# Selecting the top 256 keys of a row: a bitwise threshold search in place of rounds of eight maxima, inside a TensorE-heavy streaming encoder step

## What is computed

```python
def dsa_attend(q, qi, wi, k_all, v_all, ki_all, mask, n_sel):
    dots = einsum('bqhd,bsd->bqhs', qi, ki_all) * (D_I ** -0.5)
    score = einsum('bqh,bqhs->bqs', wi, relu(dots))
    if mask is not None:
        score = where(mask, score, NEG_BIG)
    _, sel = lax.top_k(score, n_sel)          # n_sel = 256 for the prompt
    ...                                        # attention over the selected keys only
```

## Time and profile of the kernel before

| | |
|---|---|
| runs shown | 3953.46, 3950.20, 3951.51 us |
| median | 3951.51 us |
| span of the profiled execution (first to last instruction) | 3929.5 us |
| median less span | 22.0 us |
| PE, DVE, ACT, POOL busy | 3692.2, 2321.4, 1128.6, 758.1 us |
| DVE in L1604 and L1605 (all rounds, both halves) | 367.4 and 359.9 us, plus 92 ns for each value load |

### The profile page before, as it was taken

The page is one execution under the profiler, slowest core; times in us unless marked ns, Lnnn a source line. Parts: engine busy times, 40 slices in busy tenths (PEclk is TensorE's granted clock), DMA queues, the critical chain, the costliest instruction groups (busy, mean ns, idle before and its releaser), DMA issues. The chain is left out here.

```text
span 3929.5 us, 54494 instructions
## 1 busy us (share of the span) xinstructions
PE 3692.2 (94%) x21676; PEld 2935.9 (75%) x21676; DVE 2321.4 (59%) x4713; ACT 1128.6 (29%) x2672; POOL 758.1 (19%) x812
## 2 busy tenths in 40 slices
PE   7997899999999999999999998999989999899998
PEld 5765577787877667778767787887766777688887
DVE  1664566498963664549556554488955565554542
ACT  1124333211124442321234332111134443322221
POOL 2300220301101232220100015312000101453334
PEclk9998899999999999999999999999999999999999
DMA  4331223412212222342312123343221212342223
GB/s 146 97 113 58 83 90 95 137 52 78 84 51 75 69 88 84 105 124 81 96 63 73 60 66 116 114 115 110 73 80 40 77 38 67 87 145 86 65 82 96
DMA packets 151606, 339.55 MB, mean 86 GB/s; under 512 B 30184, under 2 KB 68648, under 8 KB 138040
## 3 DMA queue, kind: packets, MB, share of 16 engines
q1 hardware_dynamic: 91576, 291.04, 23.7%
q10 hardware_dynamic: 59776, 45.02, 3.9%
HBM read 299.33 MB, written 36.68 MB: 86 GB/s over the span
## 5 line engine op out<-in xcount | busy, mean ns | idle before, releaser
L901 PE MATMUL PS<-xn,wring 128*128 128x272 f32 (+1 forms) x7168 | 1682.0, 394 | 33.9 <-DVE xn L1527 11.7
L901 PEld LDWEIGHTS PS<-xn,wring 128*128 128x128 f32 x7168 | 1374.8, 194 | 298.4 <-issue 37.4
L1859 POOL TENSOR_TENSOR xT<-xT,res 128x272 f32<-128x272 f32 (+1 forms) x320 | 253.9, 795 | 2302.9 <-ACT res L1184 2254.8
L901 PE MATMUL PS<-dense,wring 128*128 128x256 f32 (+1 forms) x2816 | 662.7, 394 | 11.9 <-DVE dense L1509 6.3
L901 PEld LDWEIGHTS PS<-dense,wring 128*128 128x128 f32 x2816 | 537.6, 194 | 111.5 <-issue 10.9
L1604 DVE MAX8 top<-scr 128x8 f32<-128x384 f32 (+6 forms) x418 | 367.4, 879 | 12.2
L1605 DVE MATCH_REPLACE8 scr<-top,scr 128x384 f32<-128x384 f32 (+6 forms) x418 | 359.9, 861 | 0.0
L1184 ACT ACTIVATE res<-PS 128x272 f32<-128x272 f32 (+1 forms) x320 | 123.2, 387 | 587.0 <-PE PS L901 565.4
L922 PE MATMUL PS<-wring,xn 128*128 128x256 f32 (+1 forms) x1152 | 267.9, 392 | 4.0 <-ACT dense L1198 4.0
L922 PEld LDWEIGHTS PS<-wring,xn 128*128 128x128 f32 (+1 forms) x1152 | 213.1, 187 | 53.6 <-issue 8.8
L901 PE MATMUL PS<-catT,wring 128*128 128x272 f32 (+1 forms) x1024 | 231.5, 387 | 5.3 <-issue 2.7
(11 more groups left out here) (199 smaller groups left out, 4113.2 us busy)
## 6 DMA issues: line engine op xcount, KB each, us to landing
wring<-in_wu SPq DMA_DIRECT2D x88, 1024.0 KB, 4.9
wring<-in_wf SPq DMA_DIRECT2D x88, 512.0 KB, 3.7
wring<-in_wo SPq DMA_DIRECT2D x64, 512.0 KB, 3.7
wring<-in_wd SPq DMA_DIRECT2D x96, 320.0 KB, 2.9
wring<-in_wd SPq DMA_DIRECT2D x64, 384.0 KB, 3.1
wring<-in_wn SPq DMA_DIRECT2D x16, 1024.0 KB, 5.3
kv<-out_projT ACTq DMA_DIRECT2D x48, 256.0 KB, 4.1
out_projT<-dense SPq DMA_DIRECT2D x40, 272.0 KB
```

Source lines behind the costliest of these rows:

```text
L901: mm = nc.tensor.matmul(PS[:, dbank(t.g0), 0:cw], wtile(t.q, i), rhs, start=(kk == a), stop=(kk == b - 1))
L1859: nc.gpsimd.tensor_tensor(x, x, res[:, i % NRES, 0:cw], ALU.add).then_inc(s_res, 1)
```

## The change

For half 1 only (m = 1 and m = 3) the pick steps go, and with them all 128 rounds of L1604 and L1605 of a stage; half 0 keeps them. The steps of X for half 1 become: load, dots, then near and far of all four units after each other (the dots of the next unit now in the "far" step; the scores are accumulated straight into the `bias` tile, so that all four units' scores lie there together), "sign", 31 steps "bit", four steps "last".

"sign" counts, for each row, the scores at or above 0 and so settles whether the 256th largest value is negative; the row is multiplied by -1 if so, and the goal count is set. The 31 "bit" steps then find the threshold's fp32 pattern: eight for the exponent, by multiplying the candidate by powers of two, and 23 for the mantissa. In each, units 0 and 1 (640 and 768 keys) are counted by DVE (a compare with the candidate and a sum, in one instruction), units 2 and 3 (896 and 1024 keys) by ACT (the sign of score minus candidate, summed along the row). DVE moves all candidates. "last" sets a last mantissa bit for the far units, restores signs, settles ties with a running count (a scan), and writes the bias. Step "bit" 15 carries the loads of stage B. `bmask`, an unused constant, makes room for `halves`, the powers 2^-1 to 2^-23.

```diff
+EXPONENTS = (127, 63, 32, 16, 8, 4, 2, 1)
+MANTISSA = 23
+BITS = len(EXPONENTS) + MANTISSA
+ON_DVE = 2
...
 def _pick_steps(h):
     out = [("load", 0, 0), ("dots", 0, 0)]
+    if h == 1:
+        for y in range(len(PICKS[h])):
+            out += [("near", y, 0), ("far", y, 0)]
+        return out + [("sign", 0, 0)] + [("bit", b, 0) for b in range(BITS)] + [("last", y, 0) for y in range(len(PICKS[h]))]
...
-ATT_LOAD = [("pick", len(PICKS[h]) - 1, 2) for h in range(2)]
+ATT_LOAD = [("pick", len(PICKS[0]) - 1, 2), ("bit", BITS // 2, 0)]
...
         for what, y, z in PICK_STEPS[h]:
-            k = PICKS[h][y].nk / 1000
+            k = PICKS[h][min(y, len(PICKS[h]) - 1)].nk / 1000
             if what == "load":
                 out.append((0, 0.5, 0, 14))
+            elif what == "sign":
+                out.append((0, 0, 6, 0))
+            elif what == "bit":
+                out.append((0, 3, 3.5, 0))
+            elif what == "last":
+                out.append((0, 0, 10 * k, 0))
...
@@ idx_tensor @@
-                elif what == "pick" and z == 6 and y + 1 < len(PICKS[h]):
+                elif what == ("far" if h == 1 else "pick") and z == (0 if h == 1 else 6) and y + 1 < len(PICKS[h]):
                     dots(y + 1, 0)
...
@@ idx_scalar @@
+                elif what == "bit":
+                    act.wait_ge(x_cand, BITS * (m // 2) + y + 1)
+                    for i in range(ON_DVE, len(PICKS[1])):
+                        u = PICKS[1][i]
+                        ins = nc.scalar.activation(rl[:u.w, i - ON_DVE, 0:u.nk], bias[:u.w, u.bias:u.bias + u.nk], ACT.Sign, bias=cand[:u.w, i:i + 1],
+                                                   accum_out=count[:u.w, i:i + 1])
+                    ins.then_inc(x_cnt, 1)
...
@@ idx_vector @@
+            def count_from(i, bound):
+                u = PICKS[1][i]
+                return nc.vector.tensor_scalar(work[:, 0:u.nk], kept(u), bound, None, ALU.is_ge, ALU.add, accum_out=count[:, i:i + 1])
+
+            def move(b, part):
+                c, hit = cand[:, part], sel[:, part]
+                step(nc.vector.tensor_tensor(hit, count[:, part], goal[:, part], ALU.is_ge))
+                e = b - len(EXPONENTS)
+                if e < 0:
...
+                    step(nc.vector.tensor_scalar(hit, hit, yes - no, no, ALU.mult, ALU.add))
+                    last = nc.vector.tensor_tensor(c, c, hit, ALU.mult)
...
+                    return last
+                step(nc.vector.scalar_tensor_tensor(hit, hit, 0.5 if e < MANTISSA - 1 else 1.0, steps_of[:, e, part], ALU.subtract, ALU.mult))
+                return nc.vector.tensor_tensor(c, c, hit, ALU.add)
...
+                elif what == "bit":
+                    if y:
+                        dve.wait_ge(x_cnt, bits + y)
+                        move(y - 1, far).then_inc(x_cand, 1)
+                    for i in range(ON_DVE):
+                        step(count_from(i, cand[:, i:i + 1]))
+                    step(move(y, near))
+                elif what == "last":
+                    if y == 0:
+                        dve.wait_ge(x_cnt, bits + BITS)
+                        step(move(BITS - 1, far))
...
+                        for i in range(ON_DVE, 4):
+                            step(count_from(i, sel[:, i:i + 1]))
...
+                    step(nc.vector.tensor_scalar(x, x, sign[:, y:y + 1], None, ALU.mult))
+                    step(nc.vector.tensor_scalar(work[:, 0:u.nk], x, bound, None, ALU.is_gt, ALU.add, accum_out=count[:, y:y + 1]))
+                    step(nc.vector.tensor_scalar(same, x, bound, None, ALU.is_equal))
+                    step(nc.vector.tensor_scalar(least[:, y:y + 1], count[:, y:y + 1], -1.0, float(TOP_P), ALU.mult, ALU.add))
+                    step(nc.vector.tensor_tensor_scan(rank, same, same, 0.0, ALU.add, ALU.max))
+                    step(nc.vector.scalar_tensor_tensor(same, rank, least[:, y:y + 1], same, ALU.is_gt, ALU.mult))
+                    step(nc.vector.scalar_tensor_tensor(rank, x, bound, same, ALU.is_lt, ALU.add))
+                    nc.vector.tensor_scalar(x, rank, 8 * NEG, None, ALU.mult).then_inc(x_bias, 1)
```

More of the change, by code:

```diff
@@ L497, in build @@
         ident, mean, hmean = sb("ident", [P, P]), sb("mean", [P, P]), sb("hmean", [P, P])
-        lmask, bmask = sb("lmask", [P, NL, 32]), sb("bmask", [P, 4, 32])
+        lmask, halves = sb("lmask", [P, NL, 32]), sb("halves", [P, MANTISSA, 4])
+        steps_of = sb("steps_of", [P, MANTISSA, 4])
+        cand, count, least, goal, sign, sel = (sb(n, [P, 4]) for n in ("cand", "count", "least", "goal", "sign", "sel"))
         epst, fgain = sb("epst", [P, 1]), sb("fgain", [P, KD])
@@ L552, in build @@
         x_in, x_dots, x_relu, x_acc, x_bias = sem("x_in"), sem("x_dots"), sem("x_relu"), sem("x_acc"), sem("x_bias")
+        x_cand, x_cnt = sem("x_cand"), sem("x_cnt")
         s_kv = [sem("s_kv0"), sem("s_kv1")]
@@ L751, in load_rest @@
             def load_rest():
-                for t, name in ((par, "params"), (fgain, "fgain"), (clow, "clow"), (ident, "ident"), (lmask, "lmask"), (bmask, "bmask"),
+                for t, name in ((par, "params"), (fgain, "fgain"), (clow, "clow"), (ident, "ident"), (lmask, "lmask"), (halves, "halves"),
                                 (hmean, "hmean")):
@@ L1582, in idx_vector, with kept @@
                     step(nc.vector.memset(bias[0:64, u.bias + u.nk - 64:u.bias + u.nk], 8 * NEG))
+            def kept(u):
+                return bias[:u.w, u.bias:u.bias + u.nk]
+            def count_from(i, bound):
[6 more added lines that the diff above has]
+                if e < 0:
+                    up = EXPONENTS[b + 1] if e < -1 else 0
+                    yes, no = 2.0 ** up, 2.0 ** (up - EXPONENTS[b])
+                    step(nc.vector.tensor_scalar(hit, hit, yes - no, no, ALU.mult, ALU.add))
+                    last = nc.vector.tensor_tensor(c, c, hit, ALU.mult)
+                    if e == -1:
+                        step(last)
+                        w = part.stop - part.start
+                        step(nc.vector.tensor_tensor(steps_of[:, :, part], halves[:, :, part], c.unsqueeze(1).to_broadcast([P, MANTISSA, w]), ALU.mult))
+                        last = nc.vector.tensor_tensor(c, c, steps_of[:, 0, part], ALU.add)
+                    return last
+                step(nc.vector.scalar_tensor_tensor(hit, hit, 0.5 if e < MANTISSA - 1 else 1.0, steps_of[:, e, part], ALU.subtract, ALU.mult))
+                return nc.vector.tensor_tensor(c, c, hit, ALU.add)
+            near, far = slice(0, ON_DVE), slice(ON_DVE, 4)
+            bits = BITS * (m // 2)
             for what, y, z in PICK_STEPS[h]:
-                u = PICKS[h][y]
-                wk = work[:u.w, 0:u.nk]
+                u = PICKS[h][y] if what not in ("bit", "sign") else None
                 if what in ("near", "far"):
+                    wk = kept(u) if h == 1 else work[:u.w, 0:u.nk]
                     for hh in range(2):
@@ L1592, in idx_vector @@
                             dve.wait_ge(x_in, 16 * sum(IX_LOADS[i % 2] for i in range(m + 1)))
-                            dve.wait_ge(x_bias, sum(len(PICKS[i % 2]) for i in range(m)) + y)
+                            dve.wait_ge(x_bias, sum(len(PICKS[i % 2]) for i in range(m)) + (y if h == 0 else 0))
                             nc.vector.tensor_scalar(wk, rl[:u.w, hh, 0:u.nk], iw[:u.w, u.slot, 0:1], None, ALU.mult).then_inc(x_acc, 1)
@@ L1600, in idx_vector @@
                         if u.prompt:
-                            step(nc.vector.memset(work[0:64, u.nk - 64:u.nk], NEG))
+                            step(nc.vector.memset(wk[0:64, u.nk - 64:u.nk], NEG))
                 elif what == "pick":
+                    wk = work[:u.w, 0:u.nk]
                     for r in range(BURST * z, min(BURST * z + BURST, ROUNDS[h][y])):
```

33 lines of the change are left out of this document (31 added, 2 removed).

## The result

The change makes the kernel faster, by about twice what was forecast: a ratio of **0.9904, 95% interval 0.9882 to 0.9926**, 3904.32 us (median of four runs, 3898.34 to 3917.21) beside 3950.86 in the same rounds. The two medians alone would give 0.988, on the edge of that interval. Forecast was 3932, about 0.995; the median lies just under the low end of the range, 3908. Rows of "before" stand above and are named by their group.

What follows compares the result with a forecast made beforehand. TensorE (PE), busy 94% of the span, bounds the kernel. B and C gaps -20, old X losses -17, new ones +18 make -19 us: span about 3910, plus 22.0 to the median, 3932; range 3908 to 3980.

Steps and rivals of the forecast that it cites:

- I let idle and clock loss shrink in proportion to steps per turn: B1, C1, B3, C3: more dense turns between steps win back 2.8, 4.0, 6.3 and 7.3 us, together 20.
- I take half: B1, C1, X3, B3, C3: half of (1 - clock) x length counted as loss, 3.0 to 6.2 us each, the rest overlapping idle.
- Rival 4: B and C: gaps shrink to the bound of 45 us, giving 3907; chance 0.09.
- X, -17 + 18: X1 and X3: old losses of 17 us go, new ones of 18 come, bounds 5 and 60.
- the old losses: X1 and X3: PE idle of 3.9 and 9.1 us and 3.8 for X3's clock, 17 us, all to go.
- (b): FFN tiles and bits of X: ACT waits for DVE in each bit; 7 us of PE idle, 3 for the clock.
- The 22.0 us between span and median: Whole kernel: 22.0 us added to the forecast span of about 3910 to reach a median of 3932.
- Rival 1: B and C gaps stay as chains within a step, X gives back its win: -1 +/- 7 us, 3950; chance 0.17.
- Rival 2: Bits of X: copies of dense tiles held up behind ACT's counts cost 56 us, net +37, 3988; chance 0.22.
- Rival 3: ACT in X1: sign needs another activation table than tanh, 16 more loads, 21 us on ACT, 3947; chance 0.05.

Runs made afterwards that it cites:

- repeat of the change: The changed kernel run once more with no edit, beside the kernel before in the same rounds: 0.9886 [0.9864, 0.9908], 3902.33 us.
- before again: The kernel before run once more with no edit, for a second profiled execution: 3949.2 us, span 3947.3.

## Why the prediction was partly right

The sign and the mechanism were right: PE's time, not DVE's, is the measure; X's lighter work is worth nothing by itself in the sum of both layers; the gain comes from more dense turns between the steps, of B in both layers and of C in the second only. The size was half of what came. Term by term:

- **"I let idle and clock loss shrink in proportion to steps per turn", -20: the step that failed.** Some 16 of the 20 were idle time, 4 were clock. Idle in B1, C1, B3 and C3 went from 64.2 to 34.8 us (repeat of the change: 2.3, 17.4, 3.7, 11.3), -29.4 where 16 stood. It was not proportional anywhere: B lost 80% of its gaps for a quarter to two fifths more turns, C3 over half, and C1, for which -4 was written, gained 10. Rival 4, "more gain", had the better argument for B (1.5 us more for a step clears most waits of at most 2.2), with a chance of only 0.09. That its time, 3907, is near the measured one is in part luck: it had C's gaps go too, and C1's grew.
- **"I take half" of the clock's loss: also too low.** In X3 to C3 (1 - clock) x length falls from 28.6 to 9.1 us, by the two-digit clocks, and PE's busy time for the same matmuls by 15.6. In the start stretch it is 37 beside 57, against 14.6 us of busy time. So some three quarters of it or more is paid. Over both layers' windows PE's busy time fell by 14.6 us in this pair of executions, where the sum had some 5 for it. In the other pair, before again and the first profile of the change, it fell by 3.5, and between the means of the three and the two by 11. So the clock is some 6 us of what was missing on the mean, and no one pair fixes it; the larger part is idle time, 25 us less in both layers where the sum had 14.
- **X, -17 + 18: right as a sum.** X1 and X3 idle 15.5 us before and 19.8 in the repeat (15 or less was the mark set, so by that mark it missed): the old losses did not all go. The parts are otherwise than written: the coupling with ACT (b), 7, shows in PE's waits with 1.6 us in X3; the norm at the edge to the FFN was not in the sum at all and went from 3.5 to 5.1 us in X3.
- **The 22.0 us between span and median** was added as if it were overhead. It is spread between executions, in the start stretch, and a fair sum would have started from the median.
- **Durations.** A count of 640 columns took 873 ns against 823, of 768 1013 against 957; ACT's pair 1035 + 1137 + 2 x 191 = 2.55 us against 2.57. DVE came to 2063.6 us (forecast 2080), ACT to 1262.2 (1288). The scans are 1491 to 2292 ns, 7.6 us a stage with the two between; by the only short row I had taken 12. The slope is (2292 - 1491) / 384 = 2.09 ns a column, twice that of a count. The Trainium skill, "DVE: opcode table, instruction layouts, handler registers and perf-mode slots", section on feedback, has the scan at half the throughput, and the estimate from that was 7: the trace agrees.
- **Rival 1, no difference: fell** with the B gaps. Its picture is the run with the old spacing, 0.9989.
- **Rival 2, slower behind ACT's copies: fell.** PE's waits for copies and relus in X3 come to 8.6 us and in X1 to 2.5, against the 20 set as the mark; a third unit on ACT brings it out only a little. That DVE can lag, its starting point, is true, but it bites when DVE carries all counts, and then at the norm and at copies that stand behind no count, as ACT has none there.
- **Rival 3, tables: fell.** The tanh's line has 8 loads instead of 7, and L1341, the sign, has none; over all lines of ACT there are 54 loads, 56 before.

Not settled: why C1 does not profit as C3 does. In the change it meets the last FFN down tiles of the first layer's first half, and 8.1 of the 9.8 us that C1 idles more than before lie in its first 77 us: 4.5 in two waits for copies of these tiles (L1204), 2.7 for DVE (L1833), 0.9 at a norm. Moving it away only moved the gaps, and more room for the sums, which is not about C, helped most.

## What to carry to other kernels

Work taken off an engine that is not the bound is worth only the room it frees: here nothing until the plan was redone, and the plan was unusable (+2.9%) without it. Do not scale short, frequent waits with crowding: here they went one by one, from 7 to 4 to 1, at their old length, and a try with part of the room shows how many. Where all following work needs an engine's result, as at a norm, its lag passes on (one wait of 14.1 us here), so look at its load just before such an edge as well as at its share of a stage. And take the gain apart by layer: a difference of nothing in the sum hid -13 and +11 us.

## What the runs showed of the hardware beyond that

- The start of the kernel, with the same instructions in both, took 616 or 630 us, at a granted clock of 0.94 or 0.91, with 74 to 75 us idle both times. Idle time repeated within 2 us in each stage between executions of one kernel, time at the lower clock level did not; 14 us of such luck are a third of the effect measured here.
- A plain in-place tensor-scalar pass with a scalar per row (L1680) took 1389 ns for 1024 columns and 918 for 640, where L1644, also in place and with a scalar per row, took 554 for 640: the four passes were counted at 2.6 us and took 4.8. What makes it slow was not tried.
